# Attention of layers 1 and 2: one block of TensorE work in each cycle, with transposes over two shared banks

## The reference

```python
# layer 1: chunked_mixer, 16 heads of 64, every token sees the chunks before it within the band
q = (h @ w_q).reshape(B, n_c, CHUNK, B_HEADS, B_HEAD_DIM)
s = einsum('bnqhd,bnkhd->bnhqk', q, k_band) * B_HEAD_DIM ** -0.5 + bias
p = softmax(where(valid, s, -inf));  o = einsum('bnhqk,bnkhd->bnqhd', p, v_band) @ w_o

# layer 2: 8 heads of block attention (softmax) and 8 heads of stick breaking
h = modulate(rms_norm_2(x, g_mix), sh_m, sc_m)
qa, ka, va, qb, kb, vb, gate_logits = split(h @ w_in)
oa = moba_attention(qa, ka, va, rel_bias)        # causal softmax here: one block of 256 tokens
z = einsum('bhqd,bhkd->bhqk', qb, kb) * scale
log_keep = where(past, log_sigmoid(-z), 0.0)
log_later = cumsum(log_keep, reverse) - log_keep
ob = where(past, exp(log_sigmoid(z) + log_later), 0.0) @ vb
x = x + gt_m * ((g_a * (oa @ w_br_moba) + g_b * (ob @ w_br_sb)) @ w_out)
```

## Time and profile before

| | us |
|---|---|
| median of 3 runs | 963.92 |
| lowest and highest | 963.77, 963.95 |
| the profiled execution | 963.82 |
| its span, first to last instruction | 961.9 |
| granted TensorE clock | 0.999 |

### The profile page before, as it was taken

How to read it: one execution, slowest core, us unless ns; L and a number is a source line. 1 busy time by engine, 2 the same in 40 slices (tenths; PEclk the granted TensorE clock), 3 DMA queues, 4 the chain that set the end, 5 groups by cost and what they waited for, 6 DMA issues and landing times.

```text
span 961.9 us, 18743 instructions
## 1 busy us (share of the span) xinstructions
PE 946.1 (98%) x7898; PEld 913.1 (95%) x7898; DVE 715.8 (74%) x1326; ACT 544.3 (57%) x845; POOL 17.8 (2%) x51
## 2 busy tenths in 40 slices
PE   9999999999999999999999999999999999999997
PEld 9889999999998988899999997998999999999996
DVE  7874897787669777699888888555655789888653
ACT  7755654444447366565444554556756576666542
POOL 0000000000000000000000000000220000000000
PEclk9999999999999999999999999999999999999999
DMA  9646376767735734168768891653344636555621
GB/s 344 227 170 241 131 279 248 237 245 269 257 132 220 262 133 150 71 232 324 277 231 302 308 341 50 257 176 121 105 142 160 219 133 220 182 211 179 219 88 44
DMA packets 28259, 195.62 MB, mean 203 GB/s; under 512 B 3216, under 2 KB 3600, under 8 KB 5264
## 3 DMA queue, kind: packets, MB, share of 16 engines
q1 hardware_dynamic: 28176, 194.43, 56.9%
HBM read 192.98 MB, written 1.05 MB: 202 GB/s over the span
## 4 chain that ended last, share of the span: by engine, by line
PE 91%; ACT 4%; DVE 3%; issue 1%; DMA 1%; SPq 0%; POOL 0%; DVEq 0%; ACTq 0%
PE bank L541 25%; PE bank L542 25%; PE bank L547 24%; PE bank L721 2%; PE bank L747 2%; PE bank L630 2%; PE bank L624 2%; PE bank L585 2%; PE bank L625 2%; PE bank L596 2%; PE bank L590 1%; ACT s_whi L992 1%; PE bank L731 1%; DMA s_front<-in_front 1%; DVE s_wlo L1480 1%
## 5 line engine op out<-in xcount | busy, mean ns | idle before, releaser
L1480 DVE TENSOR_TENSOR s_wlo<-s_raw,s_whi 128x512 fp32r<-128x512 f32 (+1 forms) x354 | 364.5, 1072 | 129.8 <-ACT s_whi L992 129.4
L992 ACT ACTIVATE s_whi<-s_raw 128x1024 fp32r<-128x1024 f32 (+2 forms) x226 | 299.9, 1354 | 199.7 <-PE bank L547 190.8
L541 PE MATMUL bank<-s_hh,s_whi 128*128 128x256 f32 x1392 | 390.2, 280 | 0.9 <-DVE s_wlo L1480 0.7
L542 PE MATMUL bank<-s_hl,s_whi 128*128 128x256 f32 x1392 | 384.7, 276 | 0.0
L547 PE MATMUL bank<-s_hh,s_wlo 128*128 128x256 f32 x1383 | 382.2, 276 | 0.0
L541 PEld LDWEIGHTS bank<-s_hh,s_whi 128*128 128x128 f32 x1392 | 261.4, 188 | 6.2 <-issue 4.2
L542 PEld LDWEIGHTS bank<-s_hl,s_whi 128*128 128x128 f32 x1392 | 261.5, 188 | 0.1
L547 PEld LDWEIGHTS bank<-s_hh,s_wlo 128*128 128x128 f32 x1383 | 259.7, 188 | 0.0
L541 PE MATMUL bank<-s_ph,s_whi 128*128 128x256 f32 x528 | 145.9, 276 | 0.0
L542 PE MATMUL bank<-s_pl,s_whi 128*128 128x256 f32 x528 | 145.7, 276 | 0.0
L547 PE MATMUL bank<-s_ph,s_wlo 128*128 128x256 f32 x525 | 144.9, 276 | 0.0
(11 more groups left out here) (264 smaller groups left out, 1290.5 us busy)
## 6 DMA issues: line engine op xcount, KB each, us to landing
s_raw<-in_gu SPq DMA_DIRECT2D x44, 1024.0 KB, 4.9
s_raw<-in_dn SPq DMA_DIRECT2D x33, 1024.0 KB, 4.9
s_raw<-in_wada SPq DMA_DIRECT2D x24, 1024.0 KB, 5.2
s_raw<-in_up SPq DMA_DIRECT2D x22, 1024.0 KB, 4.9
s_raw<-in_wo SPq DMA_DIRECT2D x8, 1024.0 KB, 5.0
s_raw<-in_win_g SPq DMA_DIRECT2D x8, 1024.0 KB, 4.9
s_raw<-in_mla SPq DMA_DIRECT2D x4, 1024.0 KB, 13.4
s_raw<-in_wkv_v SPq DMA_DIRECT2D x4, 1024.0 KB, 5.4
```

Source lines behind the costliest of these rows:

```text
L541: e.matmul(out, hi, xh[:, k, :], start=first, stop=False, skip_group_check=True)
L542: e.matmul(out, hi, xl[:, k, :], start=False, stop=False, skip_group_check=True)
L992: e.activation(whi[w % SPLIT][:, at], src, ACT.Copy).then_inc(S.hi.tick((w, c0)), 1)
L1480: e.tensor_tensor(wlo[s][:, at], src, whi[s][:, at].bitcast(F32), ALU.subtract).then_inc(S.lo.tick((i, j), (i, "all")), 1)
```

## The change

Layers 1 and 2 get a new order. `_in_blocks` takes a table with the unit at which each block stands (`BLOCKS1`, `BLOCKS2`). Block c holds the scores (or sticks) of pair c, the values of pair c - 2, and the transposes (or sums) of pair c - 1, both heads. The steps exp, scale, keep and stick stand at fixed distances behind a block. The transposes of both heads are written by `turn_both` over banks 6 and 7, four of the six in bank 6 and two in the lower half of bank 7. The values of layer 1 go to the upper half of bank 7, so that `values_out` has to know where they are. ScalarE copies the second head's transposes in two copies, as they lie in two banks. One entry of `HALVED` moves from unit 102 to unit 86 of `win_g`. Layer 0 keeps its order. In layer 2 `turn` stays as it is (banks 5 and 6), as the diff changes only layer 1's calls.

```diff
+BLOCKS1 = (21, 31, 41, 52, 62, 72, 83, 93, 106, 113)
+BLOCKS2 = (21, 31, 41, 52, 64, 81, 98, 115, 132, 147)
+
+def _in_blocks(units, blocks, pairs, soft):
+    plan = {}
+    def at(n, *steps):
+        plan.setdefault(n, []).extend(steps)
+    for c, n in enumerate(blocks):
+        if c < pairs:
+            at(n, ("scores" if c < soft else "sticks", c))
+        if 0 <= c - 2 < pairs:
+            at(n, ("values", c - 2))
+        if 0 <= c - 1 < soft:
+            at(n, ("turn", (c - 1, 0)), ("turn", (c - 1, 1)))
+        elif soft <= c - 1 < pairs:
+            at(n, ("sums", c - 1))
+            at(n + 4, ("stick", c - 1))
+        if 0 <= c - 2 < pairs:
+            at(n if c - 2 < soft else n + 2, ("chunk", c - 2))
+        if c < soft:
+            at(n + 5, ("exp", c))
+            at(n + 9, ("scale", c))
+        elif c < pairs:
+            at(n + 9, ("keep", c))
+    for n, unit in enumerate(units):
+        yield from plan.get(n, ())
+        yield unit
 def _order1():
-    return _mixed(_units("wq1") + _units("wo1"), _soft_steps(range(8)), {"wq1": 0.35, "wo1": 0.35},
-                  lambda p: ("wq1", 16 * (p // 2) + 15), "wo1")
+    return _in_blocks(_units("wq1") + _units("wo1"), BLOCKS1, 8, 8)
 def _order2():
-    return _mixed(_units("win_q") + _units("win_g"), itertools.chain(_soft_steps(range(4)), _stick_steps(range(4, 8))),
-                  {"win_q": 0.3, "win_g": 0.2}, lambda p: ("win_q", 16 * (p // 2) + 15), None)
+    return _in_blocks(_units("win_q") + _units("win_g"), BLOCKS2, 8, 4)
...
+            def turn_both(s, A, p):
+                take(6, S.soft, (s, "turned", p, 1))
+                bank_of[s, "turn", p] = (6, 7)
+                if p >= 1:
+                    q.wait_ge(S.soft, (s, "turned", p - 1, 1))
+                else:
+                    q.wait_ge(*freed[7])
+                for i in range(6):
+                    a = i // 3
+                    q.wait_ge(S.score, (s, p, "scaled", a))
+                    m = e.transpose(banks[6 + i // 4][:, i % 4 * P:(i % 4 + 1) * P],
+                                    A.S[p % 2][:, a, i % 3 * P:(i % 3 + 1) * P], ident[:, :])
+                    if i % 3 == 2:
+                        m.then_inc(S.attn.tick((s, "turn", p, a)), 1)
...
-                elif step == "turn":
-                    turn("o1", A1, *i, 6 if i[0] < 2 else (5, 6)[i[1]])
+                elif step == "turn" and i[1] == 0:
+                    turn_both("o1", A1, i[0])
                 elif step == "values":
-                    values("o1", A1, i, 64, A1.PT[i % 2], ("wkv_v", i // 4, 1), S.soft, ("o1", "turned", i, 1), 7)
+                    values("o1", A1, i, 64, A1.PT[i % 2], ("wkv_v", i // 4, 1), S.soft, ("o1", "turned", i, 1), 7, T)
...
             def turned(s, A, p, a):
-                bank = banks[bank_of[s, "turn", p, a]]
-                q.wait_ge(S.attn, (s, "turn", p, a))
+                q.wait_ge(S.attn, (s, "turn", p, 1 if (s, "turn", p) in bank_of else a))
...
+                    if a == 0:
+                        m = e.activation(to, first[:, 0:384], ACT.Copy)
+                    else:
+                        e.activation(to[:, 0:P], first[:, 384:512], ACT.Copy)
+                        m = e.activation(to[:, P:384], second[:, 0:T], ACT.Copy)
```

More of the change, by code:

```diff
@@ L109 @@
 HALVED = {("wo0", 36): (0,), ("gu0", 0): (1,), ("gu0", 4): (4,), ("gu0", 8): (4,), ("wkv_k", 0): (1,), ("wo1", 52): (0,), ("gu1", 0): (1,), ("gu1", 4): (2,),
-          ("gu1", 8): (1,), ("win_k", 0): (1,), ("win_g", 102): (0,), ("wbr", 0): (1,), ("wout", 0): (1,), ("up2", 0): (1,),
+          ("gu1", 8): (1,), ("win_k", 0): (1,), ("win_g", 86): (0,), ("wbr", 0): (1,), ("wout", 0): (1,), ("up2", 0): (1,),
           ("up2", 8): (1,)}
@@ L410, in tile_out, with values_out @@
             return banks[bank_of[name, j - j % 2]][:, (j % 2) * T:(j % 2 + 1) * T]
+        def values_out(s, p, n):
+            at = T if s == "o1" else 0
+            return banks[bank_of[s, "values", p]][:, at:at + n * T]
         def pair(bank):
@@ L732, in turn, with values @@
                 m.then_inc(S.attn.tick((s, "turn", p, a)), 1)
-            def values(s, A, p, dv, probs, v_event, p_signal, p_event, b):
-                bank = take(b, S.xlo, (s, p))
+            def turn_both(s, A, p):
[12 more added lines that the diff above has]
+                        m.then_inc(S.attn.tick((s, "turn", p, a)), 1)
+            def values(s, A, p, dv, probs, v_event, p_signal, p_event, b, at=0):
+                bank = take(b, S.xlo, (s, p))[:, at:512]
                 bank_of[s, "values", p] = b
@@ L1040, in turned @@
             def turned(s, A, p, a):
-                bank = banks[bank_of[s, "turn", p, a]]
-                q.wait_ge(S.attn, (s, "turn", p, a))
+                q.wait_ge(S.attn, (s, "turn", p, 1 if (s, "turn", p) in bank_of else a))
                 if p >= 2:
                     q.wait_ge(S.attn, (s, "values", p - 2))
+                if (s, "turn", p) in bank_of:
+                    first, second = (banks[b] for b in bank_of[s, "turn", p])
+                    to = A.PT[p % 2][:, a, :]
+                    if a == 0:
[3 more added lines that the diff above has]
+                        m = e.activation(to[:, P:384], second[:, 0:T], ACT.Copy)
+                    m.then_inc(S.soft.tick((s, "turned", p, a)), 1)
+                    return
+                bank = banks[bank_of[s, "turn", p, a]]
                 e.activation(A.PT[p % 2][:, a, :], bank[:, 0:384], ACT.Copy).then_inc(S.soft.tick((s, "turned", p, a)), 1)
             def chunk(s, A, p, n):
-                bank = banks[bank_of[s, "values", p]]
+                bank = values_out(s, p, n)
                 q.wait_ge(S.attn, (s, "values", p))
-                e.activation(A.oh[:, n * p:n * (p + 1), :], bank[:, 0:n * T], ACT.Copy).then_inc(S.xhi.tick((s, p)), 1)
+                e.activation(A.oh[:, n * p:n * (p + 1), :], bank, ACT.Copy).then_inc(S.xhi.tick((s, p)), 1)
             def tokens_out(name, g, V, R=None):
@@ L1557, in chunk @@
             def chunk(s, A, p, n):
-                bank = banks[bank_of[s, "values", p]]
                 q.wait_ge(S.xhi, (s, p))
                 to = slice(n * p, n * (p + 1))
-                src = pair(bank) if n == 2 else bank[:, 0:T].rearrange("p (a b) -> p a b", a=1)
+                src = values_out(s, p, n).rearrange("p (a b) -> p a b", a=n)
                 e.tensor_tensor(A.ol[:, to, :], src, A.oh[:, to, :].bitcast(F32), ALU.subtract).then_inc(
```

## The result

The changed kernel takes **968.57 us**, the median of five runs (966.74 to 969.84), beside 963.78 for the kernel before (963.48 to 963.95) on the same chip. The ratio is 1.0049 with an interval of 1.0038 to 1.0060: slower by 4.8 us, and 1.3 us above the top of the range. The profiled run of the changed kernel took 969.65 us with a span of 967.8.

The account below looks back on a forecast made before the run. PE, busy 98% of the span, bounds the kernel. Joins, old waits and new waits: layer 1 -1.9 - 1.3 + 4.7 = +1.5, layer 2 -1.5 - 0.8 + 2.4 = +0.1; 963.9 + 1.6 = 965.5 us, range 962.0 to 967.3.

Parts of the forecast that it names:

- What bounds the kernel: Whole kernel: PE is busy 98% of the span, so only its own instructions and its few waits can move the end.
- Joins: Attention blocks of layers 1 and 2: fewer, joined blocks save 1.9 us in layer 1 and 1.5 us in layer 2.
- my two ends: Layer 2, four sums joined to values: each saves between 0.02 and 0.10 us, with 0.05 taken.
- the slow products: Products starting late behind a block: fewer blocks save an estimated 0.6 us in layer 1 and 0.35 in layer 2.
- Old waits: PE's three waits in layer 1 and two in layer 2 go, removing 1.3 and 0.8 us.
- New waits: Transposes wait for scaled scores queued behind low and high weight parts: 4.7 us in layer 1, 2.4 in layer 2.
- the ladder of pairs 1 and 4: Layer 1: scale behind low part, high part and exp; PE waits 1.65 + 0.13 us (pair 1), 1.3 + 0.13 (pair 4).
- At nothing: Extra ScalarE copies, the moved halved product, SyncE's later wait before a load and shared bank 7 were given no cost.
- The sum: Layer 1 +1.5 us and layer 2 +0.1 us on 963.9, giving 965.5 us.
- the array pays at each change: Rival, 0.09: steps inside blocks from 64 columns or rows to a full tile pay 0.09 us each, 966.6 us.
- The delay carries over: Rival, 0.14: behind a late scale, layer 1's pairs 2, 3 and 6 are late too, +1.8 us, 967.3 us.
- No new waits: Rival, 0.10: ScalarE and VectorE have room, so joins and removed old waits are the whole effect, -5.5 us, 958.4 us.

Follow-up runs that it names:

- the fast kernel: The changed kernel with exp at n+1 instead of n+5 and scale at n+2 instead of n+9: 958.97 us, in a second run 959.12 us (ratio 0.9950).
- Experiment 7: The changed kernel with exp and scale early and each block taken apart into scores, values and transposes or sums at successive units: 962.12 us, ratio 0.9982.
- experiment 1: The changed kernel with GpSimd's select on bias2 held until the last values of layer 1: 965.37 us, ratio 1.0015.
- experiment 2: The changed kernel with scale at n+6 instead of n+9: 963.19 us; then with exp at n+1 and scale at n+2: 958.97 us, again 959.12 us.
- experiment 8: The changed kernel with small matmuls on a free bank ahead of each half of pair 7's transposes: 969.78 us, ratio 1.0060.

## Why the prediction was wrong

Point by point, by its own steps:

- **What bounds the kernel**: right. PE's busy time didn't move (946.1 to 946.5), its waits did.
- **Joins**: right within the sum, a little dear by themselves. By the prediction's measure a block of scores, values and six transposes costs 2.47 us in the fast kernel (343.52 to 346.22, less 0.23), where 2.5 was forecast. Inside a block, scores to values costs nothing (0.85 us from start to start, joined or alone). Six transposes take 0.63 behind values and 0.57 to 0.58 alone, so 0.06 is lost there, but the gap before them is saved. Sums take 1.78 behind values and 1.67 to 1.68 alone, which eats up what the join saves: 0.01 us a place is left, below the lower of my two ends (0.02), where I took 0.05. Experiment 7 gives 2.7 to 3.1 us for its joins. That is no check of my 3.4, as it takes 12 joins of scores or sticks with values apart where I had counted 9 new ones; it says that its own expectation of 3.5, made of much the same prices, was 0.4 to 0.8 too high. What the slow products are worth no run shows by itself.
- **Old waits**: right, all five gone. The fast kernel has 4.9 us of the 5.5 that joins and old waits were to give together, and 0.35 of the missing 0.6 are its two small delays.
- **New waits**: right in place, mechanism and nearly in size. By starts, as the price of a block over the same block without a wait: pair 1 of layer 1 pays 1.77 (forecast 1.78), pair 4 1.33 (1.43), pair 2 0.17 (0.17); in layer 2 pair 1 pays 1.77 (1.88), pair 2 0.34 (0.38), pair 0 0.18 (0.1). That of pair 0 stays in the fast kernel, so its cause may be another. The small ones are too short for the list of waits above. They stand in the timeline, such as that of pair 2 in layer 2, whose transposes start 1.00 us behind the values instead of 0.81:

```profile
665.04 0.87 PE L799 MATMUL bank<-s_PT,s_V 128*64 128x256 f32 x8
666.04 1.00 PE L767 MATMUL bank<-s_ident,s_S 128*128 128x128 f32 x6
```

  Pair 7 was mis-sized: 1.07 without the meeting, for 1.33. I laid the ladder of pairs 1 and 4 there, but its piece already belongs to the feed-forward behind and is made in one high part (1.92 us) and one low part (2.29) instead of two and four.
- **At nothing**: this is the step that failed. I wrote that no DMA is moved, and that SyncE's wait for the last scores moves by a microsecond in front of a load whose data isn't wanted for long, and gave that no cost. True, and beside the point: I asked who needs the data, and not what its landing starts. It starts 1.95 us on GpSimd, in the few microseconds in which VectorE scales the last pair. I never looked at GpSimd's timeline in layer 1, where in the kernel before the select began just after the last multiplication of the scaling had. What stood at nothing measured 3.2 us in the medians (experiment 1). None of my rivals had it: their delays were all in the order of the queues, and this one isn't in any queue.
- **The clock**: I priced waits at their length. 1.7 us of extra wait cost 4.5 in the profiled run, because the clock went down behind it. In the traces, waits of 1.6 and 1.1 us that stand alone (pairs 1 and 4) did not bring it down. Why it falls in some executions and not in others stays open.
- **The sum**: with the select out of the way the kernel takes 965.37 us, where 965.5 was forecast. Its terms bear that out: its new waits add up to 6.7 us for the forecast 7.1, so what joins and old waits give together there is 5.4 for the forecast 5.5. With the select, 965.4 + 1.7 + 2.8 = 969.9, near the profiled run's 969.65; the fastest run, with its clock up, is at 966.74, near 965.4 + 1.7 = 967.1. The range was built from the terms that I had, so it could not hold this one.
- **The rivals**: "the array pays at each change" did not happen at its price. The changes cost 0.06 us (values to transposes) and 0.10 (values to sums), but a block with transposes costs no more than the forecast had, and the joined sums 0.04 a place more, so its 1.1 us above the forecast did not come. The rule that I set beside it, that a change of tiling mode drains the engine (the Trainium skill, "TensorEngine Tiling (Array Packing)", Key Properties), shows nothing from 64 rows to 64 columns, and 0.06 to 0.10 us from 64 columns to a full tile. "The delay carries over" did not happen: pairs 3, 5 and 6 don't wait. "No new waits" (958.4) is what the timetable of experiment 2 brings: 959.1.

## What to carry to other kernels

Before an edit moves a load or a wait at no cost, look up what its landing or its end releases, and on which engine; an instruction of GpSimd that starts by itself when data lands can hold a short VectorE multiplication until it is over, and the place where it strikes moves with the edits. Whether that costs anything depends on how soon PE wants the result: 3.2 us in the blocks, nothing in the kernel before with its scale moved. When steps are joined to spare an engine its gaps, the time for the steps between them shrinks as well: put these at the head of their queues in the same edit, which made a loss of 0.5% into a gain of 0.5% here. A second wait close behind the first can cost more than its length.

## What the runs showed of the hardware that I had not expected

- A GpSimd select (128 x 2048 in 1.95 us, 128 x 1536 in 1.50) holds a VectorE multiplication of 128 x 128 (0.28 us alone) or 128 x 256 (0.34) that begins after it, until the select is over: 2.01, 1.48 and 1.43 us for the first, 2.03 for the second (experiment 8, whose 128 x 256 began at 385.32). A multiplication that had begun before it was not held (0.35 us), and the select then took 2.08 to 2.09 us (the kernel before, and experiment 2 with scale at n+6). A reciprocal of 128 x 4 and a subtraction of 128 x 256 with one input from a bank were not held either.
- In one traced execution two waits of PE of 0.87 and 1.64 us, with three transposes between, were followed by 6.8 us at the lower clock, at a price of 2.8 us. In another kernel's trace 0.87 and 1.60 us were not, and with matmuls in the place of most of the waiting the clock stayed up. For the executions without a trace, times and mean clocks suggest a shorter fall or none.
- Matmuls on 64 rows followed by matmuls on 64 columns cost nothing at the change; the two gaps, 0.20 us in all, are paid on entering from and leaving to the fp32r products.
